# Half modulation units issued from GpSimd's DMA queue instead of SyncE's, and their reads placed anew in the first projections

## What is computed

```python
c_act = jax.nn.silu(c)
mod = c_act @ ada_w[l] + ada_b[l]                 # 2048 -> 6 x 2048
sh1, sc1, g1, sh2, sc2, g2 = jnp.split(mod, 6, axis=-1)
h = rmsnorm(x, norm1_g[l]) * (1.0 + sc1[:, None]) + sh1[:, None]
x = x + g1[:, None] * token_mixer(h, w_in[l], ...)
h = rmsnorm(x, norm2_g[l]) * (1.0 + sc2[:, None]) + sh2[:, None]
x = x + g2[:, None] * moe_ffn(h, router_w, router_bias, exp_w_gate[l], exp_w_up[l], exp_w_down[l])
```

## Time and profile before

| | |
|---|---|
| median of 3 runs | 3067.46 us (3066.72 to 3068.49) |
| the profiled execution's own time | 3068.92 us |
| its span | 3067.1 us |
| PE busy | 2788.3 us (91%) |
| VectorE (DVE) busy | 1891.5 us (62%) |
| ScalarE (ACT) busy | 1299.4 us (42%) |
| GpSimd (POOL) busy | 24.4 us (1%) |
| mean DMA rate | 210 GB/s |

### The profile page before, as it was taken

How to read it: one execution, slowest core, us unless ns; L and a number is a source line. 1 busy time by engine, 2 the same in 40 slices (tenths; PEclk the granted TensorE clock), 3 DMA queues, 4 the chain that set the end, 5 groups by cost and what they waited for, 6 DMA issues and landing times.

```text
span 3067.1 us, 42249 instructions
## 1 busy us (share of the span) xinstructions
PE 2788.3 (91%) x16468; PEld 2409.3 (79%) x16468; DVE 1891.5 (62%) x2400; ACT 1299.4 (42%) x1609; POOL 24.4 (1%) x46
## 2 busy tenths in 40 slices
PE   2669999897899999999799898999889999999998
PEld 0248888676788787778599386999779998998996
DVE  5996765456666788988766544454554455445454
ACT  1024443343344567777433043534344543443443
POOL 0000000000000000000000000000000000000000
PEclk9779998798899999999899997999999999999999
DMA  8588666331577799999445252544444455545553
GB/s 319 227 324 287 246 251 217 123 110 46 192 255 251 264 321 363 370 368 373 191 151 178 82 185 87 187 176 172 149 175 164 177 193 183 186 179 192 187 182 124
DMA packets 144715, 644.59 MB, mean 210 GB/s; under 512 B 10923, under 2 KB 10988, under 8 KB 89048
## 3 DMA queue, kind: packets, MB, share of 16 engines
q1 hardware_dynamic: 136416, 593.53, 53.5%
q0 software_dynamic: 5344, 30.93, 2.8%
q10 hardware_dynamic: 2840, 18.56, 1.7%
HBM read 635.59 MB, written 7.39 MB: 210 GB/s over the span
## 4 chain that ended last, share of the span: by engine, by line
PE 71%; DVE 14%; DMA 8%; ACT 4%; issue 3%; DVEq 0%; ACTq 0%; SPq 0%
PE ps L1497 70%; DMA raw<-in_stream 5%; DVE raw L952 3%; DVE w_lo L869 3%; ACT w_hi L550 2%; DMA under_r<-in_stream 1%; DVE under_r L964 1%; DMA arena<-in_dft_k 1%; DVE h_lo L920 0%; DVE arena L928 0%; ACT arena L665 0%; DVE arena L1024 0%; ACT arena L571 0%; DVE arena L1037 0%; DVE arena L1417 0%
## 5 line engine op out<-in xcount | busy, mean ns | idle before, releaser
L869 DVE TENSOR_TENSOR w_lo<-raw,w_hi 128x1024 fp32r<-128x1024 f32 x968 | 1169.8, 1223 | 768.1 <-ACT w_hi L550 765.5
L550 ACT ACTIVATE w_hi<-raw 128x1024 fp32r<-128x1024 f32 x968 | 1009.4, 1056 | 779.0 <-PE ps L1497 685.4
L1497 PE MATMUL ps<-h_hi,w_hi 128*128 128x256 f32 x2944 | 843.0, 286 | 23.8 <-DVE h_lo L920 17.0
L1497 PE MATMUL ps<-h_lo,w_hi 128*128 128x256 f32 x2944 | 839.3, 285 | 0.0
L1497 PE MATMUL ps<-h_hi,w_lo 128*128 128x256 f32 x2944 | 839.0, 285 | 0.0
L1497 PEld LDWEIGHTS ps<-h_hi,w_hi 128*128 128x128 f32 x2944 | 571.9, 194 | 25.9 <-issue 24.4
L1497 PEld LDWEIGHTS ps<-h_lo,w_hi 128*128 128x128 f32 x2944 | 571.7, 194 | 0.2
L1497 PEld LDWEIGHTS ps<-h_hi,w_lo 128*128 128x128 f32 x2944 | 571.5, 194 | 0.0
L1497 PE MATMUL ps<-w_hi,r_hi 128*128 128x512 f32 x1184 | 470.2, 397 | 11.1 <-DVE w_lo L869 4.4
L1497 PE MATMUL ps<-w_lo,r_hi 128*128 128x512 f32 x1184 | 463.1, 391 | 0.0
L1497 PE MATMUL ps<-w_hi,r_lo 128*128 128x512 f32 x1184 | 462.8, 391 | 0.0
(11 more groups left out here) (266 smaller groups left out, 1925.0 us busy)
## 6 DMA issues: line engine op xcount, KB each, us to landing
raw<-in_stream SPq DMA_DIRECT2D x524, 1024.0 KB, 5.0
under_r<-in_stream SPq DMA_DIRECT2D x80, 512.0 KB, 5.7
arena<-in_mod_units ACTq DMA_DIRECT2D x16, 1024.0 KB, 4.8
filters<-arena POOLq DMA_DIRECT2D x4, 1280.0 KB, 5.7
arena<-filters POOLq DMA_DIRECT2D x4, 1280.0 KB, 6.1
x<-in_x POOLq DMA_DIRECT2D x1, 2048.0 KB, 18.9
arena<-bias_rows POOLq DMA_DIRECT2D x2, 1024.0 KB, 6.9
x<-bias_rows POOLq DMA_DIRECT2D x2, 1024.0 KB, 10.4
```

The costliest lines, as they stand in the source:

```text
L550: act.activation(dst, src, ACT.Copy).then_inc(hi_ready, 1)
L869: dve.tensor_tensor(low, src, high, ALU.subtract).then_inc(lo_ready, 1)
L1497: return pe.matmul(o, a, b, start=start, stop=stop)
```

## The change

The chunks are issued by POOL, in the queue of the small tables. SP's woven order goes: it issues weights alone.

```diff
+TOEPLITZ_AT = (7, 8, 13, 14)
...
-            counts.append(1 if k % 3 < 2 else 0)
+            counts.append(0 if k % 4 == 3 or k in TOEPLITZ_AT else 1)
```

```diff
-            aside(0)
-            aside(1)
-            weight(4)
-            used = 0
-            for k in range(len(ASIDE)):
-                if k % 2 == 0:
-                    weight(k // 2 + 5)
-                for _ in range(ASIDE[k]):
-                    aside(used + 2)
-                    used += 1
-            for n in range(len(ASIDE) // 2 + 5, BASE["moe"]):
+            for n in range(SLOTS, BASE["moe"]):
                 weight(n)
```

```diff
+            def aside(first, last):
+
+                for j in range(first, min(last, ASIDE_HALVES)):
+                    if j >= 2:
+                        pool.wait_ge(sem("aside_done"), j - 1)
+                    pool.dma_start(aside_slot[:, j % 2, :], d["stream"][FIRST_UNITS + j // 2][:, j % 2 * HALF:(j % 2 + 1) * HALF])\
+                        .then_inc(sem(f"aside_landed{j % 2}"), 16)
+
+            def issued(k):
+
+                return sum(ASIDE[:k]) + 2
+            aside(0, issued(0))
             pool.wait_ge(sem("brow_stored"), 16)
...
+            load("ld_sink", (stat[:, 32:40], d["sinks"].partition_broadcast(P)))
+            aside(issued(0), issued(7))
             toeplitz(0, toep)
+            aside(issued(7), issued(13))
             toeplitz(2, toep2)
-            load("ld_sink", (stat[:, 32:40], d["sinks"].partition_broadcast(P)))
+            aside(issued(13), issued(56))
             pool.wait_ge(sem("att_out"), 16 * 2)
+            load("ld_cmp", (w1k, d["w1k"]), (w1v, d["w1v"]), (w2c, d["w2kv"]), (peT, d["pe"]))
+            aside(issued(56), issued(62))
             toeplitz(1, toep2)
-            load("ld_cmp", (w1k, d["w1k"]), (w1v, d["w1v"]), (w2c, d["w2kv"]), (peT, d["pe"]))
+            aside(issued(62), issued(74))
             pool.wait_ge(sem("cmp_hidden"), 2)
             toeplitz(3, toep)
+            aside(issued(74), ASIDE_HALVES)
             pool.wait_ge(sem("att_out"), 16 * 3)
```

## The result

The changed kernel took 3082.39 us (median of 7 runs, 3074.03 to 3087.32) beside 3068.50 us for the kernel before (7 runs): a ratio of 1.0040, interval 1.0025 to 1.0055. It is slower by 0.4%, some 12 us (13.9 by the medians). The forecast was 3065.3 us with a range up to 3074.0; the result is outside. The profiled execution took 3086.29 us (span 3084.5).

A forecast was written before the change was run, and what follows sets the result against it. PE was taken to bound the plain steps, and the series of VectorE and ScalarE work the attention rounds. Terms -2.5 + 0 + 0.3 = -2.2 us, from a median of 3067.46, gave 3065.3 us; range 3059.5 to 3074.

The forecast's parts named there:

- The reads are placed anew: Steps 0 to 70 and the gap before the third attention: moving reads to other steps costs nothing, worth 0.
- I take 5.0: the ln_g row: Chunks from POOL's queue land in 5.0 us, estimated from a half-MB POOL load of 4.3 us; under 5.4 suffices.
- The -2.5 us: Attention rounds: VectorE's four waits for chunks, 2.48 us in all, go when chunks land in under 5.4 us.
- the four places: Chunk waits inside attention rounds: 0.94 and 0.48 us in the first stage, 0.36 in the second, 0.70 in the third.
- POOL's issues: 80 issues come to POOL at 0.54 to 0.92 us each, on an engine idle 99% of the span: directly 0.
- Tables and chunks in one queue: Step 58's chunk behind the compression tables: 1.0 us of stall in place of 1.07, counted as 0.
- Toeplitz 3: Third attention, second round: the table moves just ahead of the fourth round's chunks, costing 0 to 1.5 us, taken as +0.3.
- nothing moves: Rival: chunk landing follows the engines' whole load, stays at 6.3 us, and the time at 3067.5 us; 5%.
- Late everywhere: Rival: POOL's chunks land at 7.4 us, 15 attention reads wait 2.0 us each, about 3095 us; 7%.
- The clock: Rival: shorter gaps avoid PE's clock drops from 330 and 425 us, 5.2 us faster, 3060.1 us; 12%.
- the rival with the tables: Steps 58 to 62: a very late chunk behind the tables stops PE 6.1 us, clock drops, 3073.8 us; 10%.
- no wait for a chunk in the second and fourth round: Sign of being right, in the first attention: VectorE no longer waits for chunks in these two rounds.

The follow-up runs named there:

- experiment 1: The kernel before with only the new table of reads (three in four steps); SP still issues chunks behind weights: ratio 1.0039 to the kernel before.
- experiment 6: experiment 1 with a third slot for chunks, in a part of arena free until the gap: ratio 0.9995 to the kernel before.
- experiment 8: experiment 1 with each step's chunks issued ahead of the weight, still two slots: ratio 0.9994 to the kernel before.
- experiment 9: The changed kernel with a third slot for chunks, POOL still issuing them: 3072.80 us beside 3073.76 for the kernel before, ratio 0.9997.
- experiment 4: The kernel before, old table, with SP issuing each step's chunks ahead of the weight: ratio 0.9988 to the kernel before.
- experiment 3: The changed kernel with Toeplitz and compression tables issued by SP between its weights, POOL issuing chunks alone: ratio 1.0032 to the kernel before.
- experiment 2: The changed kernel with the old table of reads (two steps of three); chunks and tables stay in POOL's queue: ratio 1.0025 to the kernel before.
- experiment 7: The kernel before, old table, with a third chunk slot and chunks issued ahead of the weight: 3067.34 us beside 3073.02, ratio 0.9981.

## Why the prediction was wrong, point by point

- **"The reads are placed anew ... Worth 0"** is the main failure. The distance had been worked out: with three reads in four steps the third chunk is asked for 4.6 us before it is wanted, where the old rule always leaves three steps, 3 x 2.88 - 1.2 = 7.4 us. But it was set against a hoped-for landing of 5.0 us and called 0.4 us that the lead absorbs. The row that was at hand has chunks landing in 5.6 us (median) to 12.1, 1 us or more over the 4.6. In experiment 1 the third read of every group waits, by 1.84 us or more, and beside the tables by 8.78. The term, measured alone, is +0.39% (about 12 us), and experiments 6, 8 and 9 show that it works through this distance: one more slot or a shorter way brings the time back to that of the kernel before, with the same reads at the same steps. The longest landing was used as a bound for one chunk at steps 58 to 62, and not for the rule that decides how often such a landing hurts.
- **"I take 5.0: the ln_g row"** failed. The chunk issued beside a weight took 6.5 us (288.97 to 295.44) for 6.3 before, and the reads in the first attention waited 0.77 and 0.85 us for 0.94 and 0.48. The -2.5 us did not come. At the second attention VectorE waits 2.70 and 2.17 us instead of 0.36, but these are the new table's doing: the first is the read of step 46, the third of a group of three, and the second, at step 49, waits in every kernel that has the new table ahead of it, two slots and not the order of experiment 4 (0.96 to 2.17 us in four kernels), and in none with the old one. The ln_g load was the nearest row by size and engine, but nothing says that it shared with a weight issued just ahead of it. This stretch of the changed kernel (queues, then landings) shows why there was nothing to win:

```profile
q0 software_dynamic: 286, 1.04, 38.8%
q1 hardware_dynamic: 144, 1.05, 34.8%
...
raw<-in_stream SPq DMA_DIRECT2D x1, 1024.0 KB, 6.2
under_r<-in_stream POOLq DMA_DIRECT2D x2, 512.0 KB, 6.2
```

  The two queues move equal bytes in the same time and end together: two chunks of 0.5 MB in POOL's, one weight of 1 MB in SP's. In one queue the weight took 4.8 us and the chunks 6.3. The second queue delayed the weight, which nobody waits for, and brought the chunks no earlier. The Trainium skill (DMA: Bandwidth & Descriptors, "Issuing engines are not separate DMA queues") was quoted for just this and then set aside with "what the four places lack is latency, not bandwidth". The trace agrees with the page.
- **POOL's issues, "directly 0"**: no time by themselves, but a delay. POOL starts 0.30 us after a read ends in the shown case (288.67 to 288.97), where SP needed 0.03 (287.64 to 287.67). Small, and in every chunk. Its issues were not stretched: each chunk's took 0.53 to 0.57 us.
- **Tables and chunks in one queue, 0**: the place named had a gap of 0.94 us for 1.0 expected, and by the path described: the chunk landed 7.6 us after its request, for 7.0. But the same mechanism struck one table later, at Toeplitz 1: 11.0 us for the chunk behind it, a gap of 2.63 us and a clock of 0.67 after it. Experiments 3 and 9 show that it adds little to the table's cost.
- **Toeplitz 3, +0.3**: right in size; the chunk issued behind it waited 0.80 us (0 at that read before).
- **The rivals**: "nothing moves" was right about the landing and wrong about the time. "Late everywhere" had the sign and the late chunks, at 6 to 7 us, but priced them in the attentions alone. The clock took the other way: around and behind the new gaps at 408.22 and 488.87 it fell to 0.52 and 0.67, which is up to 5 x (0.21 + 0.48 + 0.33) = 5 us of PE at full speed lost, of the 7 us that the clock lost more than before. Only the rival with the tables had priced such a drop, for its one gap.
- **The signs**: of those for being right, "no wait for a chunk in the second and fourth round" and "PE full in the plain steps" failed. Of those for being wrong, none came at the place named; the gap of over 2 us on PE came at 488.87, behind the window of 452 to 466 us.
- **Right**: SP's relief brought nothing that shows (experiment 9 has it too and is at 0.9997); weights that land later hold up nobody (no ScalarE wait for `raw` in any kernel, at up to 8.4 us in the first attention); the gap before the third attention stays at 15.5 us.

What stays open is how much of experiment 2's 0.25% comes from chunks behind tables and how much from later requests. Its trace points at the tables, since most of the delay stands ahead of the first attention, where the gap of 4.66 us is; POOL's queue for the chunks with the old rule and the tables in SP's was not run. Open too is why halved weights let chunks beside tables land sooner and chunks beside a weight in the attention not.

## What to carry to other kernels

For data that streams through few slots, work out for each read the time from the read that frees its slot to its own, and set the longest landing of that stretch against it; the average rate says nothing, and a denser pattern in a table of reads shortens just this distance. If it is short, buy slots, or issue the urgent transfer first in its queue; a second queue beside a loaded one did neither here. And when a landing time is taken from a neighbouring row, take one that had the same traffic ahead of it.

## What the runs showed that was not expected

- Waits for chunks are not worth the same everywhere: removing 26 us of the 31.9 (experiment 7) gave 0.19%, while adding 16 to 22 us (experiment 1, the changed kernel) cost 0.4%. They are free up to the lead of three steps, and then dear: a 4.70 us gap on PE brought a clock of 0.57 and 0.75 in the stretches around and behind it.
- A chunk behind one table of 1 MB in rows of 1 KB in the same queue took 11.0 to 14.4 us, about twice its way beside a weight (6.5).
